# Cached keys turned by VectorE in place in an attention step: the load that feeds it, and the values beside it

## The chip, the cores and the metric

The kernel runs on 1 core of one Trainium2 chip. The metric is device time in microseconds (us), the median of the runs. Before the change it is 2017.1 us over 3 runs (2013.8 to 2017.39).

## What is computed

One step of a four-layer model for a prompt of 256 positions and for 8 samples of 8 positions each. Every layer has a mixer and then a cross attention over 256 memory positions; the change is in the attention, and there in the samples' part, whose keys and values are cached in HBM per sample.

```python
D_MODEL = 1024; DEPTH = 4; DEC_BATCH = 8; DEC_SEQ = 8; N_MEM = 256; X_HEADS = 4; X_HEAD_DIM = 256

def memory_cross_attn(x, mem_k, mem_v, w_q, w_o):
    bsz, L, _ = x.shape
    q = (x @ w_q).reshape(bsz, L, X_HEADS, X_HEAD_DIM)
    s = jnp.einsum('blhd,bmhd->bhlm', q, mem_k.astype(q.dtype)).astype(F32) * (X_HEAD_DIM ** -0.5)
    p = jax.nn.softmax(s, axis=-1).astype(x.dtype)
    o = jnp.einsum('bhlm,bmhd->blhd', p, mem_v.astype(x.dtype)).reshape(bsz, L, D_MODEL)
    return o @ w_o
...
    # in reference(): 'cache_mem_k', 'cache_mem_v' have shape (DEPTH, DEC_BATCH, N_MEM, X_HEADS, X_HEAD_DIM)
    y_sample, ... = run_trunk(x_sample, cache_mem_k, cache_mem_v, ...)
```

## The kernel before

Everything is float32. A projection's weights come in blocks of 256 columns (1024x256, four transfers of 256 KB each, issued by `put`, line 425) into four slots `raw`. ScalarE writes each half block's high part to `wh` (line 1713), GpSimd the rest to `wl` (line 1693), and TensorE makes three products per tile (lines 773, 774, 778); one such half block is called a unit. Memory keys and values of the prompt are made from `raw` directly (lines 1458 and 1467).

The order of the work on each engine is written out by hand; engines wait for each other by counted semaphores. All weights, caches and states are loaded by transfers that SyncE (SP) issues in its program order, and a wait there holds up all that is behind it.

The attention of a layer, on TensorE: the prompt's memory keys; eight query units (`project`, t = 0 to 7), each scaled out of PSUM by VectorE (line 2929); the prompt's scores (`prompt_scores`, line 1541); then the samples' scores from sixteen cached key blocks of 128 positions x 1024 columns (two blocks per sample). Since a key block comes with positions on the partitions and the product needs the columns of a head there, `turn_cache` (line 1524) turns it by eight TensorE transposes into PSUM banks 4 and 5. ScalarE copies bank 4 (line 2187) and VectorE bank 5 (in `copy`, line 2258) into one of two buffers `at_kbt`, and `cache_scores` (line 1534) multiplies. Key block n + 1 is turned ahead of the scores of block n, and the turns of the prompt's probabilities (`prompt_turn`, line 1552) stand in between:

```python
                for n in range(1, 16):
                    turn_cache(n)
                    cache_scores(n - 1)
                    if n in (5, 6, 11, 12):
                        prompt_turn(n // 8, (n - 5) % 6)
                cache_scores(15)
```

Then follow the prompt's outputs (line 1571), part of the next layer's memory values (`values`, line 1467, not in the last layer), the turn of the samples' probabilities (line 1581), and the sixteen cached value blocks (line 1602, four products each), and at last the output projection, eight units.

The 32 cached blocks of a layer (keys 0 to 15, values 16 to 31) are loaded by `cache(n)` (line 647) as one transfer of 128 rows of 4096 bytes each. They share buffers, a ring of twelve (`KB_SLOT`), plus three more: a block is issued when the block before it in its buffer has been used (`at_kb_used`). Twelve key blocks are issued ahead of the scores, the other four and the values during them, as buffers come free.

Of the kernel before, what the change touches and what calls it, by code (L numbers as in the profile page):

```python
# [26 lines left out]
P = 128  # L27
D = 1024
# [99 lines left out]
def trunk(nc, A, RES):  # L128
    with ExitStack() as ctx:
# [249 lines left out]
        at_kbt = c(2, KD, P)  # L379
# [18 lines left out]
        at_kb += [work[:, 5120:6144], work[:, 0:D], work[:, D:2 * D]]  # L398
        KB_SLOT = [n % CACHED for n in range(28)] + [CACHED, CACHED + 1, CACHED + 2, 28 % CACHED]

        def cached_count(L, n):

            return 16 * (L * KB_SLOT.count(KB_SLOT[n]) + KB_SLOT[:n + 1].count(KB_SLOT[n]))
# [10 lines left out]
        def _(sp):  # L414
# [217 lines left out]
            def attention(layer, stores=None):  # L632

                def cache(n):
# [7 lines left out]
                    elif slot == CACHED:  # L642
                        for h in range(2):
                            sp.wait_ge(*past(f"at_k_out{h}", 32 * (layer + 1)))
                    elif slot > CACHED:
                        sp.wait_ge(*past("at_cs_full", 16 * (layer + 1)))
                    sp.dma_start(at_kb[slot], src).then_inc(S(f"at_kb_in{slot}"), 16)
# [36 lines left out]
                for n in range(SQUARES, CACHED):  # L684
                    cache(n)
                if layer:
# [3 lines left out]
                    store_keys(1)  # L690
                sp.wait_ge(*past("h_ready", KD * (2 * layer + 2)))
                for n in range(EARLY, SQUARES):
                    cache(n)
# [10 lines left out]
                for n in [*range(CACHED, 16), 28, *range(16, 28), 29, 30, 31]:  # L704
                    cache(n)
# [26 lines left out]
        def _(pe):  # L732
# [16 lines left out]
            def low(half, j):  # L749
                assert units.n % 2 == half  # L750
                return wl[:, units.n // 2 % SLOTS, j, half * P:(half + 1) * P]
# [691 lines left out]
            def attention(L):  # L1443
                def memory(n):
# [10 lines left out]
                    for k in range(KD):  # L1455
                        if n == 0:
                            pe.wait_ge(*past("mem_normal", 2 * KD * L + k + 1))
                        mm = pe.matmul(ps[:, n % 4, 0:NMEM], raw[:, block % SLOTS, k, n % 2 * P:(n % 2 + 1) * P], memh[:, k, :],  # L1458
# [58 lines left out]
                def turn_cache(n):  # L1517
                    kb = cached(n)
                    for g in range(2):
                        if n:  # L1520
                            pe.wait_ge(*past(f"at_kbt{g}_ready", seen + n))
                        for j in range(4):
                            c = 4 * g + j
                            mm = pe.transpose(ps[:, 4 + g, j * P:(j + 1) * P], kb[:, c * P:(c + 1) * P], ident[:])  # L1524
                        mm.then_inc(S("at_kb_used" if g else "at_kbt_full"), 1)

                def cache_scores(n):
                    b, a = n // 2, n % 2
                    pe.wait_ge(*past("at_kbt0_ready", seen + n + 1))
                    pe.wait_ge(*past("at_kbt1_ready", seen + n + 1))  # L1530
                    at = 256 * (b // 4) + P * a
                    for c in (0, 2, 4, 6, 1, 3, 5, 7):
                        rows = slice(32 * (c // 2), 32 * (c // 2) + 32)
                        mm = pe.matmul(ps[rows, 7, at:at + P], at_qz[:, b, c, :], at_kbt[:, n % 2, c, :],
                                       start=(n == 0 and c % 2 == 0), stop=(n == 15 and c % 2 == 1), skip_group_check=True)
                    mm.then_inc(S("at_cs_full"), 1)
# [8 lines left out]
                def prompt_turn(T, g):  # L1545

                    pe.wait_ge(*past("at_pp_ready", 2 * L + T + 1))
                    if T or g:
                        pe.wait_ge(*past("at_ppt_read", 4 * L + 2 * T + g))
                    for h in range(2):  # L1550
                        for a in range(2):
                            mm = pe.transpose(ps[:, 6, (2 * h + a) * P:(2 * h + a + 1) * P], at_pp[:, 2 * g + h, a * P:(a + 1) * P], ident[:])
# [21 lines left out]
                if L < DEPTH - 1:  # L1574
                    pe.wait_ge(*past("at_kbt1_ready", seen + 16))
# [9 lines left out]
                pe.wait_ge(*past("at_kbt0_ready", seen + 16))  # L1585
# [1472 lines left out]
```

## Time and profile before

| | |
|---|---|
| runs | 2017.1 us median of 3 (2013.8 to 2017.39) |
| span of the profiled execution | 2015.7 us |
| the profiled execution's own time, beside its span | not given apart from it; the median is 1.4 us above the span |
| TensorE busy (matmul) | 1951.5 us, 97% |
| VectorE / ScalarE / GpSimd busy | 62% / 46% / 50% |
| share of the 16 DMA engines | 49.8% (queue q1), 321.49 MB |
| HBM read / written | 292.16 MB / 29.61 MB |
| samples' scores of layer 0 (lines 1524, 1534, 1552) | from 346.56 to 376.91 us |

Times in the trace count from the start of the span. A row of the chain of waits gives the start, the duration and what the end of the kernel waited for at that time; matmuls overlap, so a row there gives the time by which a group moved the chain on. A float32 matmul is two records of the trace. In a table of windows, the share is that of 16 DMA engines and GB/s what they moved together.

### The profile page before, as it was taken

How to read it: one execution, taken by the hardware profiler on the slowest of the kernel's cores; microseconds unless marked ns; L12 is line 12 of the kernel's file. 1: busy time of each engine (PE TensorE's matmuls, PEld its weight loads, DVE VectorE, ACT ScalarE, POOL GpSimd, SP SyncE). 2: the span in 40 equal slices, each digit the busy share in tenths (PEclk: the TensorE clock that was granted, in tenths of full speed). 3: DMA queues.
4: the chain of work that ended last, by engine and by line, in shares of the span. 5: the costliest groups of instructions: out<-in, count | busy, mean ns of one | idle time of the engine just before them, and what ended most of it. 6: DMA issues, size and time to landing. Idle time of an engine off the chain costs nothing.

```text
span 2015.7 us, 35615 instructions
## 1 busy us (share of the span) xinstructions
PE 1951.5 (97%) x13890; PEld 1763.9 (88%) x13890; DVE 1244.4 (62%) x2220; ACT 930.6 (46%) x1557; POOL 1008.8 (50%) x1249
## 2 busy tenths in 40 slices
PE   7999999999999999999999999999999999999997
PEld 5998989798888988897889999999998889989976
DVE  5988342426887787755147777777454157874552
ACT  3676522334555555342354444443243347674333
POOL 4776704026555655250356666566631337776602
PEclk8999999999999999999999999999999999999998
DMA  4444476535444544487353444444586344445870
GB/s 130 149 147 135 135 250 231 208 105 174 124 116 132 151 132 140 138 297 241 113 170 108 130 130 130 137 136 146 165 313 211 132 148 141 135 148 166 292 231 27
DMA packets 332615, 324.64 MB, mean 161 GB/s; under 512 B 19768, under 2 KB 313056, under 8 KB 332448
## 3 DMA queue, kind: packets, MB, share of 16 engines
q1 hardware_dynamic: 330944, 321.49, 49.8%
q8 instruction: 111, 1.82, 0.4%
q10 hardware_dynamic: 1504, 0.87, 0.2%
q14 instruction: 56, 0.46, 0.1%
HBM read 292.16 MB, written 29.61 MB: 160 GB/s over the span
## 4 chain that ended last, share of the span: by engine, by line
PE 75%; DVE 14%; ACT 5%; issue 2%; DMA 2%; POOL 1%; SPq 1%; DVEq 0%; ACTq 0%
PE ps L773 10%; PE ps L774 10%; PE ps L778 10%; PE ps L1458 5%; PE ps L1467 4%; PE ps L1261 3%; PE ps L1524 2%; PE ps L888 2%; PE ps L763 2%; PE ps L765 2%; PE ps L764 2%; ACT wh L1713 2%; DVE work L2543 2%; PE ps L1602 1%; PE ps L1541 1%
## 5 line engine op out<-in xcount | busy, mean ns | idle before, releaser
L1693 POOL TENSOR_TENSOR wl<-raw,wh 128x256 fp32r<-128x256 f32 x1216 | 1003.3, 860 | 979.1 <-ACT wh L1713 978.9
L1713 ACT ACTIVATE wh<-raw 128x1024 fp32r<-128x1024 f32 x304 | 311.8, 1053 | 202.1 <-PE ps L778 49.8
L773 PE MATMUL ps<-Hh,wh 128*128 128x320 f32 x1200 | 372.2, 324 | 2.8 <-DVE work L2563 0.9
L774 PE MATMUL ps<-Hl,wh 128*128 128x320 f32 x1200 | 360.4, 314 | 0.0
L773 PEld LDWEIGHTS ps<-Hh,wh 128*128 128x128 f32 x1200 | 230.0, 192 | 11.3 <-DVE work L2427 2.3
L774 PEld LDWEIGHTS ps<-Hl,wh 128*128 128x128 f32 x1200 | 230.4, 192 | 2.1
L2258 DVE TENSOR_SCALAR work<-ps 128x512 f32<-128x512 f32 (+8 forms) x220 | 100.3, 474 | 170.9 <-PE ps L871 39.8
L778 PE MATMUL ps<-Hh,wl 128*128 128x320 f32 x1200 | 201.1, 310 | 0.0
L778 PEld LDWEIGHTS ps<-Hh,wl 128*128 128x128 f32 x1200 | 183.2, 189 | 0.1
L773 PE MATMUL ps<-Oh,wh 128*128 128x320 f32 x512 | 152.2, 310 | 3.7 <-DVE Ol L3004 3.7
L774 PE MATMUL ps<-Ol,wh 128*128 128x320 f32 x512 | 151.1, 308 | 0.0
L763 PE MATMUL ps<-Oh,wh 128*128 128x320 f32 x400 | 125.6, 314 | 2.0 <-DVE gate_area L2563 0.9
L764 PE MATMUL ps<-Ol,wh 128*128 128x320 f32 x400 | 123.0, 308 | 0.0
L765 PE MATMUL ps<-Oh,wl 128*128 128x320 f32 x400 | 123.0, 308 | 0.0
L2315 DVE TENSOR_TENSOR work<-work 128x320 f32<-128x320 f32 x80 | 41.2, 515 | 131.9 <-ACT work L2220 105.7
L1458 PE MATMUL ps<-work,raw 128*128 128x256 f32 x512 | 113.8, 379 | 0.0
L1467 PE MATMUL ps<-raw,work 128*128 128x256 f32 x512 | 113.3, 379 | 0.0
L1467 PEld LDWEIGHTS ps<-raw,work 128*128 128x128 f32 x512 | 96.8, 190 | 13.4
L1458 PEld LDWEIGHTS ps<-work,raw 128*128 128x128 f32 x512 | 96.5, 190 | 13.5
L773 PEld LDWEIGHTS ps<-Oh,wh 128*128 128x128 f32 x512 | 96.1, 188 | 4.7 <-DVE Ol L3004 4.7
L774 PEld LDWEIGHTS ps<-Ol,wh 128*128 128x128 f32 x512 | 96.0, 187 | 0.0
L2187 ACT ACTIVATE work<-ps 128x512 f32<-128x512 f32 x64 | 38.4, 600 | 111.7 <-PE ps L1524 111.7
(439 smaller groups left out, 3922.0 us busy)
## 6 DMA issues: line engine op xcount, KB each, us to landing
raw<-rg_w_in SPq DMA_DIRECT2D x128, 256.0 KB, 3.5
raw<-hg_w_in SPq DMA_DIRECT2D x128, 256.0 KB, 4.8
raw<-ssd_w_in SPq DMA_DIRECT2D x96, 256.0 KB, 3.9
work<-cache_mem_k SPq DMA_DIRECT2D x40, 512.0 KB, 6.3
work<-cache_mem_v SPq DMA_DIRECT2D x40, 512.0 KB, 5.1
raw<-rg_w_out SPq DMA_DIRECT2D x64, 256.0 KB, 3.6
raw<-x_w_k SPq DMA_DIRECT2D x64, 256.0 KB, 3.6
raw<-x_w_v SPq DMA_DIRECT2D x64, 256.0 KB, 3.7
```

The costliest lines, as they stand in the source:

```text
L763: pe.matmul(out, high(*wi), mh, start=start, stop=False)
L764: pe.matmul(out, high(*wi), ml, start=False, stop=False)
L765: return pe.matmul(out, low(*wi), mh, start=False, stop=stop)
L773: pe.matmul(ps[:, bank, 0:n], high(half, k), mh[:, k, 0:n], start=(k == 0), stop=False)
L774: pe.matmul(ps[:, bank, 0:n], high(half, k), ml[:, k, 0:n], start=False, stop=False)
L778: mm = pe.matmul(ps[:, bank, 0:n], low(half, k), mh[:, k, 0:n], start=False, stop=(k == 7))
L1261: mm = pe.matmul(out, x[:, k, t0:t0 + P], w(k), start=(k == 0 and n == 0), stop=(k == KD - 1 and n == 2))
L1458: mm = pe.matmul(ps[:, n % 4, 0:NMEM], raw[:, block % SLOTS, k, n % 2 * P:(n % 2 + 1) * P], memh[:, k, :], start=(k == 0), stop=(k == KD - 1))
L1467: mm = pe.matmul(ps[:, bank, 256 * a:256 * a + 256], memh[:, k, a * P:(a + 1) * P], raw[:, block % SLOTS, k, :], start=(k == 0), stop=(k = ...
L1693: ins = pool.tensor_tensor(out, src, wh[:, parted(n) % HALVES, r:r + 2].bitcast(F32), ALU.subtract)
L1713: act.activation(wh[:, nx.n % HALVES], raw[:, slot, :, half * P:(half + 1) * P], ACT.Copy).then_inc(hi_ready, 1)
L2258: return ts(out, src, 1.0, None, MUL)
```

## The change

Keys. A cached key block comes as four transfers, one for each quarter (64 columns) of every head. Quarter q of a head goes to partitions 32q to 32q + 31. Partition 32q + j receives from positions 4j to 4j + 3 the 64 columns of that quarter of each head: 16 pieces of 256 bytes. VectorE then turns 32x32 blocks in place (`turn_keys`), with a step of two words between the elements of a row. After this each partition holds two columns (even and odd) of all heads, and the score product reads them as they lie. The columns of a head are thus split into even and odd instead of the first and the second 128, so the query weights and the memory-key weights are read with a step of two words as well (`by_head`, `unit_of`), and the prompt's keys are put back in order as they are copied out (`take_keys`).

Positions. The turn leaves the 128 positions of a block in the order 0, 4, 8, ..., then 1, 5, ...; so the values' transfer reads its source rows in that order, `(j a) c -> a j c` with a = 4: still one transfer of 128 rows of 4096 bytes.

Order. `turn_cache` and its two copies go. Fourteen key blocks (not twelve) have buffers ahead of the scores, since the two halves of `at_kbt` became buffers. VectorE turns two blocks behind each of the first seven query tiles, the last two in the score stage. The four turns of the prompt's probabilities go to banks 4, 5, 6, 4 and are copied out by ScalarE, not VectorE.

```diff
-        at_kbt = c(2, KD, P)
+        kb13, kb14 = c(D), c(D)
...
+        KEYS = 14
+        RING = [*range(EARLY), *range(SQUARES, CACHED), EARLY, CACHED + 1, CACHED + 2]
+        KB_SLOT = RING + RING[0:2] + RING[2:] + [CACHED] + RING[0:3]
...
+        def unit_of(v, n):
+            half = n % 2
+            if any(q <= n < q + KD for q in Q_AT):
+                return v.rearrange("p k (x e) -> p k x e", e=2)[:, :, :, half]
+            return v[:, :, half * P:(half + 1) * P]
+        def turned_keys(slot):
+            return at_kb[slot].rearrange("p (r j e) -> p r e j", j=32, e=2)
...
-                    sp.dma_start(at_kb[slot], src).then_inc(S(f"at_kb_in{slot}"), 16)
+                    if n < 16:
+                        keys = src.rearrange("(j a) (h q x) -> q j (a h) x", a=4, h=XH, q=4)
+                        for q in range(4):
+                            to = at_kb[slot][32 * q:32 * q + 32].rearrange("p (r x) -> p r x", r=4 * XH)
+                            sp.dma_start(to, keys[q]).then_inc(S(f"at_kb_in{slot}"), 16)
+                    else:
+                        sp.dma_start(at_kb[slot], src.rearrange("(j a) c -> a j c", a=4)).then_inc(S(f"at_kb_in{slot}"), 16)
...
-                for n in [*range(CACHED, 16), 28, *range(16, 28), 29, 30, 31]:
+                for n in [28, *range(KEYS, 28), 29, 30, 31]:
                     cache(n)
...
-                turn_cache(0)
                 pe.wait_ge(*past("at_qz_ready", L + 1))
-                for n in range(1, 16):
-                    turn_cache(n)
-                    cache_scores(n - 1)
-                    if n in (5, 6, 11, 12):
-                        prompt_turn(n // 8, (n - 5) % 6)
-                cache_scores(15)
+                for n in range(16):
+                    cache_scores(n)
+                    if n in (4, 12):
+                        prompt_turn(n // 8, 0)
+                        prompt_turn(n // 8, 1)
...
+                def turn_keys(n):
+                    slot = KB_SLOT[n]
+                    wait(f"at_kb_in{slot}", cached_count(L, n))
+                    dve.transpose(turned_keys(slot), turned_keys(slot)).then_inc(S("at_kb_turned"), 1)
...
                     ts(at_q[:, t], ps[:, t % 4, 0:NT], 256.0 ** -0.5, None, MUL).then_inc(S("at_q_ready"), 1)
+                    if t < KEYS // 2:
+                        turn_keys(2 * t)
+                        turn_keys(2 * t + 1)
```

TensorE's order in layer 0, from the prompt's scores on. Before (lines 1541 scores of the prompt, 1524 turns of key blocks, 1534 their scores):

```order
L1541 MATMUL ps<-work 128x256 x16
L1524 MATMUL ps<-ident,work 128x128 x16
L1534 MATMUL ps<-work 32x128 x8
L1524 MATMUL ps<-ident,work 128x128 x8
L1534 MATMUL ps<-work 32x128 x8
L1524 MATMUL ps<-ident,work 128x128 x8
L1534 MATMUL ps<-work 32x128 x8
```

And with the change (1558 scores of the prompt, 1551 scores of key blocks, 1569 turns of the prompt's probabilities, 1586 its outputs):

```order
L1558 MATMUL ps<-work 128x256 x16
L1551 MATMUL ps<-work 32x128 x40
L1569 MATMUL ps<-ident,work 128x128 x8
L1551 MATMUL ps<-gate_area,work 32x128 x8
L1551 MATMUL ps<-cache_area,work 32x128 x40
L1551 MATMUL ps<-work 32x128 x16
L1569 MATMUL ps<-ident,work 128x128 x8
L1551 MATMUL ps<-work 32x128 x24
L1586 MATMUL ps<-work 128x256 x16
```

The scores of all sixteen blocks follow each other, with the prompt's turns after the fifth and the thirteenth.

SP's order in the same place. Before (line 425 weights, 647 cached blocks, 454 and 660 results):

```order
L647 DMA cache_area<-cache_mem_k 128x1024 x5
L647 DMA work<-cache_mem_k 128x1024
L454 DMA out_mv<-work 128x2x1024
L425 DMA raw<-x_w_v 128x2x256 x4
L425 DMA raw<-x_w_o 128x2x256 x12
L647 DMA work<-cache_mem_k 128x1024 x4
L647 DMA work<-cache_mem_v 128x1024 x2
L647 DMA gate_area<-cache_mem_v 128x1024
```

And with the change (444 weights, 668 keys, 670 values, 473 results):

```order
L668 DMA cache_area<-cache_mem_k 32x16x64 x20
L668 DMA work<-cache_mem_k 32x16x64 x12
L473 DMA out_mv<-work 128x2x1024
L444 DMA raw<-x_w_v 128x2x256 x4
L444 DMA raw<-x_w_o 128x2x256 x12
L670 DMA work<-cache_mem_v 128x1x1024
L668 DMA work<-cache_mem_k 32x16x64 x8
L670 DMA work<-cache_mem_v 128x1x1024 x3
L670 DMA gate_area<-cache_mem_v 128x1x1024
```

Eight blocks stand ahead of the weights in place of six, value block 28 comes ahead of the last two key blocks, and each key block is four transfers.

VectorE's order at the end of the query units, with the change (2946 scales a query tile, 2940 turns a key block; before, the scalings followed each other):

```order
L2940 STREAM_TRANSPOSE cache_area<-cache_area 128x16x2x32
L2940 STREAM_TRANSPOSE work<-work 128x16x2x32
L2946 TENSOR_SCALAR work<-ps 128x320
L2940 STREAM_TRANSPOSE work<-work 128x16x2x32 x2
L2946 TENSOR_SCALAR work<-ps 128x320
L2270 TENSOR_SCALAR work<-work 128x2x8x8 x4
L2963 TENSOR_REDUCE smallc<-ps 128x4
```

These are the last of the seven pairs; each pair stands between two query tiles, and TensorE waits for a tile three units later. The last tile, the placing of the samples' queries (2270) and the prompt's maximum (2963) come behind all fourteen turns.

## Rows read from the trace of the kernel before

**Rows 1.** The page, busy us (share of the span) xinstructions.
```profile
PE 1951.5 (97%) x13890; PEld 1763.9 (88%) x13890; DVE 1244.4 (62%) x2220; ACT 930.6 (46%) x1557; POOL 1008.8 (50%) x1249
```
**Rows 2.** Chain of waits in layer 0, 330 to 420 us: start us, us, what.
```profile
339.39 7.17 PE ps L1541 x32
...
370.74 0.59 PE ps L1552 x4
...
372.77 1.02 PE ps L1524 x8
373.80 0.57 PE ps L1534 x16
...
376.91 7.11 PE ps L1571 x32
...
391.36 5.32 PE ps L1602 x96
...
397.05 1.91 PE ps L1602 x32
```
**Rows 3.** The same chain in the last layer, 1915 to 1975 us.
```profile
1914.84 7.17 PE ps L1541 x32
...
1952.09 7.11 PE ps L1571 x32
...
1966.83 1.91 PE ps L1602 x32
```
**Rows 4.** The DMA view: packets, then transfers xcount, KB each, us to landing.
```profile
DMA packets 332615, 324.64 MB, mean 161 GB/s; under 512 B 19768, under 2 KB 313056, under 8 KB 332448
...
work<-cache_mem_v SPq DMA_DIRECT2D x40, 512.0 KB, 5.1
...
work<-state_rglru_conv SPq DMA_DIRECT2D x16, 24.0 KB
...
out_rgc_p<-work SPq DMA_DIRECT2D x16, 3.0 KB
out_rgh_p<-work SPq DMA_DIRECT2D x16, 1.0 KB
out_rgh_s<-work SPq DMA_DIRECT2D x16, 8.0 KB
...
work<-ssd_w_in SPq DMA_DIRECT2D x1, 128.0 KB, 3.6
...
smallc<-ssd_d SPq DMA_DIRECT2D x1, 16.0 KB, 2.4
```
**Rows 5.** Windows: us, engines busy (x instructions), granted clock, DMA share, GB/s.
```profile
259.00:261.00 2.00, 2.00 (x11) 1.77 (x10) 2.00 (x6) 0.96 (x3) 0.00 (x0) 1.00 1.01 412
...
350.00:360.00 10.00, 9.18 (x127) 6.80 (x127) 7.77 (x16) 3.74 (x9) 0.00 (x0) 1.00 0.92 323
...
380.00:381.00 1.00, 1.00 (x6) 0.90 (x5) 0.00 (x0) 0.00 (x0) 0.00 (x0) 1.00 0.95 385
...
1034.00:1035.00 1.00, 1.00 (x8) 1.00 (x8) 0.00 (x0) 0.00 (x0) 1.00 (x2) 1.00 0.56 171
```
**Rows 6.** Lines 425 and 647: issue ns min/median/max; landing of cached blocks.
```profile
L425 SPq DMA_DIRECT2D raw<-rg_w_a x32: 551/609/624, 39.0 to 1781.8; - x32
...
DMA to landing us min/median/max: 3.4/5.5/12.3
```
**Rows 7.** VectorE: a query tile in order of time; the nearest operation of 1024 elements.
```profile
909.54 0.49 DVE L2929 TENSOR_SCALAR work<-ps 128x320 f32<-128x320 f32 x1 [3.03 <-PE ps L778]
...
L2567 DVE TENSOR_TENSOR work<-work 128x1024 f32<-128x1024 f32 x8 | 10.9, 1369 | 2.3 <-ACT work L1907 2.3
```
**Rows 8.** Windows near the start, columns as in rows 5.
```profile
25.00:30.00 5.00, 2.89 (x12) 1.79 (x12) 5.00 (x7) 3.49 (x8) 5.00 (x6) 1.00 0.00 0
...
40.00:42.00 2.00, 2.00 (x9) 2.00 (x9) 1.97 (x8) 1.48 (x5) 0.00 (x0) 0.50 0.26 71
42.00:44.00 2.00, 2.00 (x14) 2.00 (x13) 1.89 (x8) 1.51 (x5) 0.00 (x0) 0.84 0.70 190
```

More of the change, by code:

```diff
@@ L397, in trunk, with by_head @@
         CACHED = len(at_kb)
-        at_kb += [work[:, 5120:6144], work[:, 0:D], work[:, D:2 * D]]
-        KB_SLOT = [n % CACHED for n in range(28)] + [CACHED, CACHED + 1, CACHED + 2, 28 % CACHED]
+        at_kb += [work[:, 5120:6144], kb13, kb14]
+        KEYS = 14
+        RING = [*range(EARLY), *range(SQUARES, CACHED), EARLY, CACHED + 1, CACHED + 2]
+        KB_SLOT = RING + RING[0:2] + RING[2:] + [CACHED] + RING[0:3]
         def cached_count(L, n):
-            return 16 * (L * KB_SLOT.count(KB_SLOT[n]) + KB_SLOT[:n + 1].count(KB_SLOT[n]))
+            landings = [64 if m < 16 else 16 for m in range(32)]
+            same = [m for m in range(32) if KB_SLOT[m] == KB_SLOT[n]]
+            return L * sum(landings[m] for m in same) + sum(landings[m] for m in same if m <= n)
+        def by_head(v, half):
+            return v.rearrange("p (x e) -> p x e", e=2)[:, :, half]
+        def unit_of(v, n):
[5 more added lines that the diff above has]
+            return at_kb[slot].rearrange("p (r j e) -> p r e j", j=32, e=2)
+        TURN_BANK = (4, 5, 6, 4)
         at_m = smallc[:, 288:352].rearrange("p (a b) -> p a b", b=8)
@@ L683, in attention @@
                     query(1)
-                for n in range(SQUARES, CACHED):
+                for n in range(EARLY, EARLY + 2):
                     cache(n)
@@ L690, in attention @@
                     store_keys(1)
+                for n in range(EARLY + 2, EARLY + 5):
+                    cache(n)
                 sp.wait_ge(*past("h_ready", KD * (2 * layer + 2)))
-                for n in range(EARLY, SQUARES):
+                for n in range(EARLY + 5, KEYS):
                     cache(n)
@@ L750, in low @@
                 assert units.n % 2 == half
+                if any(q <= units.n < q + KD for q in Q_AT):
+                    return by_head(wl[:, units.n // 2 % SLOTS, j, :], half)
                 return wl[:, units.n // 2 % SLOTS, j, half * P:(half + 1) * P]
@@ L1515, in cached @@
                     return at_kb[KB_SLOT[n]]
[L1517 to L1525, printed above, removed]
                 def cache_scores(n):
                     b, a = n // 2, n % 2
-                    pe.wait_ge(*past("at_kbt0_ready", seen + n + 1))
-                    pe.wait_ge(*past("at_kbt1_ready", seen + n + 1))
+                    pe.wait_ge(*past("at_kb_turned", seen + n + 1))
+                    keys = turned_keys(KB_SLOT[n])
                     at = 256 * (b // 4) + P * a
@@ L1708, in split @@
                 n = PARTED[nx.n]
-                slot, half = n // 2 % SLOTS, n % 2
+                slot = n // 2 % SLOTS
                 act.wait_ge(landed[slot], 64 * (n // 8 + 1))
@@ L2956, in prompt_scale @@
                             ins.then_inc(S("at_pp_ready"), 1)
[L2958 to L2960 removed]
                 prompt_max(0)
[L2963 to L2979 removed]
+                prompt_scale(0)
+                prompt_max(1)
+                if L < DEPTH - 1:
+                    memory_norm(L + 1, range(0, 4))
+                prompt_scale(1)
+                for n in range(KEYS, 16):
+                    turn_keys(n)
+                if L < DEPTH - 1:
+                    memory_norm(L + 1, range(4, KD))
+                wait("at_kb_used", 32 * L + 16)
                 did(dve.tensor_reduce(at_m[:, 5, 0:2], ps[:, 7, :].rearrange("p (b m) -> p b m", b=2), axis=AX, op=MAX))
```

64 lines of the change are left out of this document (20 added, 44 removed).

## The prediction

> **What bounds the kernel now.** I read the page first. TensorE is busy 97% of the span [rows 1], so only time taken from TensorE's queue, or a wait put into it, can move the end. The change sits in the attention part, which runs four times, so next I read the chain of waits through that part of layer 0 [rows 2]. It runs on TensorE without a break: the prompt scores (L1541) end at 339.39 + 7.17 = 346.56 us. I call this moment T. Then the sixteen cached key blocks are turned (L1524) and multiplied (L1534), and at 376.91 the prompt's outputs (L1571) begin. At 391.36 the sixteen cached value blocks are multiplied (L1602), the last of them ending at 397.05 + 1.91 = 398.96. So the key blocks take 376.91 - 346.56 = 30.35 us, and the value blocks end at T + 52.4. In the last layer [rows 3] T is 1922.01 and the value blocks end at 1968.74, T + 46.7, since no memory values for a next layer stand between. Layers 1 and 2 repeat layer 0 shifted in time.
>
> **What leaves TensorE.** At its steady pace a key block costs 1.02 us of turning and 0.57 of scores, and a turn of the prompt's probabilities 0.59 [rows 2]. The order of the changed program shows the sixteen score groups and four prompt turns alone. That is 16 x 0.57 + 4 x 0.59 = 11.5 us in place of 30.35, so 18.9 us less per layer and 75 us over four. Part of it is stalls behind the copies out of the turned banks, which go too. ScalarE's sixteen copies become four and VectorE's sixteen go; both were beside TensorE's work.
>
> **What VectorE gets.** Fourteen turns of 128x1024 stand two by two behind the query tiles, and two more inside the score stage. No row shows such a turn. The nearest is another operation of the same 1024 elements, 1.37 us [rows 7]. From below I take a copy's pace, 0.49 us for 320 elements, hence 1.0 or so with the fixed part spread; from above, twice 1.37. I take 1.37, the row with the same size. Between two query tiles VectorE now works 0.49 us and idles 3.03, a period of 3.52 [rows 7]; 0.49 + 2 x 1.37 = 3.23 fits, so the turns cost nothing as long as one is under (3.52 - 0.49)/2 = 1.5 us and the key blocks have landed. The strided reads (every second word, for the q and k weights and the turned keys) I cost at nothing: ScalarE's and GpSimd's splits run ahead, and no row of a step of two says otherwise. The range has to carry this.
>
> **What the DMA queue gets.** A key block is now 2048 pieces of 256 bytes in four transfers. The rate per engine is GB/s over share over 16. It is 412/1.01/16 = 25.5 and 385/0.95/16 = 25.3 for whole 4096-byte rows at their best, 323/0.92/16 = 21.9 when all engines are crowded, and 171/0.56/16 = 19.1 for 512-byte pieces, which is 27 ns a piece [rows 5]. A 256-byte piece costs between half of that and all of it, so a block takes 1.7 to 3.5 us of all engines against 1.3 now. Fourteen blocks come before T in about 90 us, so at most 31 us of work is added to a stretch in which the engines still have room; I take no cost. Issuing is dearer: the transfers whose source rows are cut finer (128 KB, L425) take 0.609 us of SP each [rows 6], so a key block takes 2.4 us of SP. Blocks 14 and 15 are issued after T, ahead of the values.
>
> **The values are the term that decides.** Their transfer still moves 128 rows of 4096 bytes, but the source is now read as 4 groups of 32 rows, because the turned order of the positions needs it. What does that do to the engines? The packets tell. The profile counts 19768 packets under 512 bytes [rows 4]. Of these 1408 are data: 1024 pieces of 128 bytes for one ssd_w_in transfer, and 3 x 128 for ssd_d and its two like. That leaves 18360 over 1231 transfers, the sum of the counts in that view. If each transfer put one closing packet on all 16 engines there would be 19696. Suppose instead it runs on the largest number up to 16 that divides its rows: 12 for the 80 transfers of 24 rows, 8 for 32 of 8 rows, 3 for 40 of 3 rows, 1 for 16 of one row, 16 for the other 1063. This gives 960 + 256 + 120 + 16 + 17008 = 18360, exactly. So a transfer is cut along its outermost count only, in equal parts, and never inside it (one row of 1 KB stays on one engine). The new source's outermost count is 4. An equal cut of both sides along it goes to 4 engines and no further.
>
> The Trainium skill ("DMA: Bandwidth & Descriptors", section on why a DMA increments its semaphore by 16 and not by 1) says this outright: the number is the largest up to 16 that divides the slowest count of both access patterns, and they are always the lowest-numbered engines. By it the values run on the same four engines; were the on-chip side alone to count (128 rows), it would be 16 and the whole change a gain of 75 us. The trace agrees for equal counts; no row has sides that differ.
>
> **The sum.** On four engines one value block takes 131072 bytes / 25.4 GB/s = 5.16 us, and blocks queue behind each other on the same four. After T: 0.6 us until key block 0 is used, 8 issues x 0.61 = 4.9, one value issue 0.3, then the fixed part of a landing, 3.4 us at the fastest [rows 6] less its 1.3 of data = 2.1. One value block (28) goes ahead of T; the other fifteen follow: 15 x 5.16 = 77.4. With 0.5 for the last block's products the stage ends at T + 85.8. Against T + 52.4 that is +33.4 us in layers 0 to 2, against T + 46.7 it is +39.1 in layer 3: +139 together. The 18.9 us saved ahead become waiting and are lost. One more term is TensorE's clock, since it works 0.5 us of each 5 in that wait. Early in the kernel a stretch with 2.89 us busy of 5 is still granted 1.00, and later stretches show 0.50, half speed (1.2 of 2.4 GHz). The stretch 42 to 44 us has 0.84, which puts the rise at 42.6 [rows 8]. Matmuls had stood close from about 39 us, so some 3.6 us of dense work ran at half speed and lost 1.8; four times, +7. So span 2015.7 + 146 = 2162; the median of the runs lies 1.4 above the span shown, hence 2163.
>
> **Rival 1, faster: the values still use all engines** (the on-chip side decides, or successive blocks go to different fours). Then a block takes 1.3 to 1.5 us, the sixteen are there when TensorE arrives, and the layers keep 18.9 us each: 2017 - 75 = 1942. For it: rows 4 prove the cut only where both sides agree. Against it: a cut into 16 equal parts of 4 groups would have to go inside the outermost count, which 3 rows and 1 row show it doesn't. It decides from about seven engines up: (52.4 - 8.4)/15 = 2.9 us a block is break-even.
>
> **Rival 2, slower still: the turn isn't hidden.** At 2.7 us a turn, seven tiles each take 0.49 + 5.5 - 3.52 = 2.4 us longer, T comes 17 us later in each layer, and on top of the values that is 2163 + 68 = 2231. For it: no row prices the turn. Against it: it would be dearer than any elementwise row of its size.
>
> **How the numbers follow.** The four-engine case has 0.78, rival 1 0.17, rival 2 0.04, something between (a wait I don't see, near today's time) 0.01. The four-engine case's own range: down to 2140 without the fixed parts, with cheaper issues and no clock loss; up to 2213 if each engine gives only the crowded 21.9 GB/s (5.99 us a block, +12.4 a layer), a little more if small pieces hold up weights. Eight in ten is then 2125 to 2225, which leaves out rival 1 and most of rival 2. A change of 0.2%, 4 us, is about what a measurement of this kernel can tell from none; no case lands there by itself. Faster 0.17, within 0.2% 0.01, slower 0.82.
>
> **What would show it.** Right: L1524's successor gone, key scores from T to about T + 12; then TensorE waiting some 55 us a layer on the landings of the values, one block every 5.2 us, the DMA share near 0.25 with about 100 GB/s there, the granted clock at 0.50; and 153144 packets under 512 bytes: 1408, the 131072 key pieces, and 18360 + 192 x 16 (more key transfers) - 64 x 12 (values on 4 engines, not 16). On 16 engines it would be 153912. Wrong: a DMA share near 0.9 and 300 GB/s after T and no wait on values; or VectorE's turns near 2.7 us with TensorE waiting on the query tiles.

## The result and the profile after

The changed kernel took 2231.5 us (median of 4 runs, 2228.5 to 2235.4), the kernel before 2015.4 us on the same chip: a ratio of 1.107, 95% interval 1.104 to 1.109. Forecast was 2163 us, 2125 to 2225. The direction was right, the size was 68 us short and outside the range.

The page of the changed kernel, with busy shares and the shares of the chain that ended last:

```profile
span 2233.7 us, 34475 instructions
...
PE 1945.7 (87%) x13378; PEld 1736.5 (78%) x13378; DVE 1267.2 (57%) x2204; ACT 903.5 (40%) x1509; POOL 1009.8 (45%) x1249
...
PE 54%; DMA 16%; DVE 14%; SPq 8%; ACT 5%; issue 3%; ACTq 0%; DVEq 0%
```

TensorE has 512 matmuls fewer than in [rows 1] and 87% in place of 97%. A sixth of the chain that sets the end is now DMA, and 8% is SyncE's issuing. The DMA view counts the packets:

```profile
DMA packets 457794, 324.57 MB, mean 145 GB/s; under 512 B 153144, under 2 KB 446432, under 8 KB 457632
```

153144 is the number forecast for values on four engines (153912 on sixteen). So where the two sides of a transfer have unequal outermost counts, here 4 and 128, which no row of before has, the smaller one set the number. The value stage of layer 0, from the timeline of TensorE (start us, us, what, and in brackets the idle time ahead and what ended it):

```profile
394.85 1.08 PE L1614 MATMUL ps<-cache_area,work 128*32 128x256 f32 x8 [4.35 <-DMA cache_area<-cache_mem_v]
399.84 1.08 PE L1614 MATMUL ps<-cache_area,work 128*32 128x256 f32 x8 [3.91 <-DMA cache_area<-cache_mem_v]
404.83 1.08 PE L1614 MATMUL ps<-cache_area,work 128*32 128x256 f32 x8 [3.91 <-DMA cache_area<-cache_mem_v]
```

One block every 4.99 us (5.16 forecast), and TensorE waits 3.9 us of it. The windows of the same stage and of what follows, columns as in [rows 5]:

```profile
390.00:440.00 50.00, 11.87 (x90) 2.32 (x86) 0.42 (x1) 0.77 (x2) 0.00 (x0) 0.53 0.30 114
...
452.00:454.00 2.00, 2.00 (x10) 2.00 (x9) 0.00 (x0) 0.00 (x0) 2.00 (x4) 0.51 0.00 0
454.00:456.00 2.00, 2.00 (x15) 2.00 (x15) 0.00 (x0) 0.23 (x1) 2.00 (x4) 1.00 0.00 0
```

Share 0.30 (0.25 forecast), 114 GB/s (100 forecast), clock 0.53: half speed (1.2 GHz) while TensorE mostly waits. Its matmuls stand close again from 450.31 us, the clock is still 0.51 from 452 to 454, and 1.00 from 454 on.

So much was in the prediction. What was not is mostly ahead of T. The table gives for each layer the time from the attention part's first matmul (L1458, now L1485) to T, the end of the prompt's scores, and from T on; every entry is the start or end of the first or last matmul of the line named.

| | before, L0 / L1 / L2 / L3 | after, L0 / L1 / L2 / L3 |
|---|---|---|
| start to T (L1541, now L1558) | 94.4 / 68.3 / 66.6 / 66.8 | 97.6 / 80.1 / 80.2 / 80.9 |
| T to end of key scores (L1534, now L1551) | 30.4 / 30.4 / 30.4 / 30.1 | 21.5 / 15.5 / 15.2 / 15.0 |
| T to end of values (L1602, now L1614) | 52.4 / 52.4 / 52.4 / 46.7 | 98.6 / 93.2 / 91.6 / 89.8 |

T comes 3.2 + 11.7 + 13.7 + 14.1 = 42.7 us later in all. How that happens stands in the timelines of layer 1. SyncE's queue (start us, us, what it issues), where before the first five key blocks took 2.66 us:

```profile
906.54 15.35 SPq L668 DMA_DIRECT2D work<-cache_mem_k  x20
921.94 2.75 SPq L668 DMA_DIRECT2D gate_area<-cache_mem_k  x4
...
929.54 10.49 SPq L668 DMA_DIRECT2D cache_area<-cache_mem_k  x8
940.08 1.89 SPq L683 DMA_DIRECT2D out_mk<-work  x1
...
946.41 0.47 SPq L683 DMA_DIRECT2D out_mk<-work  x1
```

and VectorE's:

```profile
944.71 0.69 DVE L2270 TENSOR_SCALAR work<-ps 128x512 f32<-128x512 f32 x1 [2.38 <-DMA out_mk<-work]
953.14 0.69 DVE L2270 TENSOR_SCALAR work<-ps 128x512 f32<-128x512 f32 x1 [7.74 <-DMA out_mk<-work]
954.20 1.76 DVE L2943 MEMSET work<- 128x2048 f32 x1 [0.37 <-issue]
955.89 0.43 DVE L2946 TENSOR_SCALAR work<-ps 128x320 f32<-128x320 f32 x1
956.23 2.36 DVE L2940 STREAM_TRANSPOSE work<-work 128x1024 f32<-128x1024 f32 x2
958.51 0.45 DVE L2946 TENSOR_SCALAR work<-ps 128x320 f32<-128x320 f32 x1
...
974.41 0.45 DVE L2946 TENSOR_SCALAR work<-ps 128x320 f32<-128x320 f32 x1
```

Eight key blocks (32 transfers) stand ahead of the first two stores of new keys (out_mk). They take 15.35 + 2.75 + 10.49 = 28.6 us of SyncE's time, where in the kernel before eleven blocks stand there and take 5.8. VectorE's last copy of keys waits 7.74 us for the second store to land, so the query tiles start late, and then each takes 2.65 us with its two turns (955.89 to 958.51) until the last at 974.41, on which TensorE waits. That wait costs once more. The prompt's scores before, after, and the window in the middle of them:

```profile
913.61 7.17 PE L1541 MATMUL ps<-work 128*128 128x256 f32 x32 [0.58 <-DVE work L2929]
...
974.92 9.47 PE L1558 MATMUL ps<-work 128*128 128x256 f32 x32 [4.12 <-DVE work L2946]
...
976.00:978.00 2.00, 2.00 (x6) 1.62 (x5) 0.00 (x0) 0.92 (x1) 0.00 (x0) 0.50 1.09 350
```

TensorE had idled 4.12 us and runs at half speed (1.2 GHz) at first. In layers 2 and 3 the same scores take 8.86 us each, so 5.7 of the 42.7 us are this clock.

### The profile page after: what moved, and what is told of

Its sections match the earlier page's. It is cut to its first block, busy times and chain, and to the rows that moved or that the text cites. A ratio compares the mean times of both kernels' runs of the same rounds, so it can differ in the third digit from the quotient of the medians.

```text
span 2233.7 us, 34475 instructions
## 1 busy us (share of the span) xinstructions
PE 1945.7 (87%) x13378; PEld 1736.5 (78%) x13378; DVE 1267.2 (57%) x2204; ACT 903.5 (40%) x1509; POOL 1009.8 (45%) x1249
## 2 busy tenths in 40 slices
DMA packets 457794, 324.57 MB, mean 145 GB/s; under 512 B 153144, under 2 KB 446432, under 8 KB 457632
## 4 chain that ended last, share of the span: by engine, by line
PE 54%; DMA 16%; DVE 14%; SPq 8%; ACT 5%; issue 3%; ACTq 0%; DVEq 0%
DMA work<-cache_mem_v 9%; PE ps L800 8%; PE ps L801 7%; PE ps L805 7%; SPq L668 5%; DMA cache_area<-cache_mem_v 4%; PE ps L1494 3%; PE ps L1288 3%; PE ps L790 2%; SPq L444 2%; PE ps L792 2%; PE ps L791 2%; ACT wh L1724 2%; DVE work L2423 2%; DVE work L2555 1%
## 5 line engine op out<-in xcount | busy, mean ns | idle before, releaser
L800 PE MATMUL ps<-Oh,wh 128*128 128x320 f32 x512 | 160.9, 325 | 8.9 <-DVE work L2946 3.9
L801 PE MATMUL ps<-Ol,wh 128*128 128x320 f32 x512 | 158.5, 321 | 0.0
L790 PE MATMUL ps<-Oh,wh 128*128 128x320 f32 x400 | 126.6, 317 | 2.0 <-DVE gate_area L2575 0.9
L2270 DVE TENSOR_SCALAR work<-ps 128x64 f32<-128x64 f32 (+7 forms) x140 | 45.6, 353 | 145.7 <-DMA out_mk<-work 41.6
L791 PE MATMUL ps<-Ol,wh 128*128 128x320 f32 x400 | 123.8, 310 | 0.0
L1614 PE MATMUL ps<-work 128*32 128x256 f32 x320 | 36.7, 561 | 97.7 <-DMA work<-cache_mem_v 96.5
L1485 PE MATMUL ps<-work,raw 128*128 128x256 f32 x512 | 113.8, 379 | 0.0
L800 PEld LDWEIGHTS ps<-Oh,wh 128*128 128x128 f32 x512 | 102.1, 199 | 12.4 <-DVE Ol L3014 5.3
L1485 PEld LDWEIGHTS ps<-work,raw 128*128 128x128 f32 x512 | 99.6, 196 | 10.5
L1494 PEld LDWEIGHTS ps<-raw,work 128*128 128x128 f32 x512 | 96.7, 190 | 14.1 <-ACT work L2147 0.6
```

The lines of the kernel that those rows point to most:

```text
L790: pe.matmul(out, high(*wi), mh, start=start, stop=False)
L791: pe.matmul(out, high(*wi), ml, start=False, stop=False)
L800: pe.matmul(ps[:, bank, 0:n], high(half, k), mh[:, k, 0:n], start=(k == 0), stop=False)
L801: pe.matmul(ps[:, bank, 0:n], high(half, k), ml[:, k, 0:n], start=False, stop=False)
L1485: mm = pe.matmul(ps[:, n % 4, 0:NMEM], by_head(raw[:, block % SLOTS, k, :], n % 2), memh[:, k, :], start=(k == 0), stop=(k == KD - 1))
L1494: mm = pe.matmul(ps[:, bank, 256 * a:256 * a + 256], memh[:, k, a * P:(a + 1) * P], raw[:, block % SLOTS, k, :], start=(k == 0), stop=(k = ...
```

## The experiments

All times are medians of 4 or more runs beside the kernel before (2015 to 2020 us); intervals are of the ratio. In e2, e3, e5, e8, e11 and e13 keys or values lie out of place, so they do the same work on other numbers and serve for timing alone. "T" in the text is the time from start to T, mean over layers 1 to 3: 67.2 us before, 80.4 after.

**The values alone, both ways.** In the changed kernel, one transfer over all rows, with ScalarE writing the probabilities in the natural order:

```diff
-    sp.dma_start(at_kb[slot], src.rearrange("(j a) c -> a j c", a=4)).then_inc(...)
+    sp.dma_start(at_kb[slot], src).then_inc(...)
...
-    act.activation(at_p[:, hb, :], ps[:, 7, ...], ACT.Exp, ...)
+    act.activation(at_p[:, hb, :].rearrange("p (h j a) -> p h a j", h=2, a=4),
+                   ps[:, 7, ...].rearrange("p (h a j) -> p h a j", h=2, a=4), ACT.Exp, ...)
```

> The changed kernel with its value blocks read in natural order again, as one transfer of 128 source rows; ScalarE puts the samples' probabilities back in order of position as it writes them (same instructions, a step of four words in the write). Theory A (a source read as 4 groups of rows runs on 4 DMA engines, and the values queue there): the 53 us a layer of waiting on values go, TensorE waits on no value load, the DMA share after T is again near 0.9, packets under 512 bytes are 153912 and not 153144, time 1985 to 2010 us (what is left is the later T, 43 us together, against 15 us or so a layer saved in the score stage). Rival B (values are late because SP issues them late, behind eight key transfers and a full queue, whatever their shape): still 30 us or more a layer of waiting on values, time over 2150 us.

And in the kernel before, only the values as 4 groups of 32 rows:

> The kernel before with only the value blocks' source read in 4 groups of 32 rows. The positions of the values no longer agree with the probabilities (the samples' attention is another sum); same work. Theory A: value stage ends about T + 92 instead of T + 52 in layers 0 to 2 and about 45 us later in layer 3, with TensorE's clock at half in the wait: 2170 to 2200 us, a value block every 5 us, DMA share 0.25. Rival B (only the issue and the key pieces matter): 2010 to 2025 us.

Measured: 1993.2 us, ratio 0.988 (0.986 to 0.991), and 2203.5 us, ratio 1.092 (1.089 to 1.094). The source access of sixteen value blocks a layer is worth 238 us in the one kernel (2231.5 - 1993.2) and 185 in the other (2203.5 - 2018.4 beside it). e1 fell in its range, e2 4 us above its own. In e1 TensorE waits for no value load: 22 to 24 us from the end of the key scores to the end of the values in layers 0 to 2 (77 in the changed kernel). A value block's issue, median 0.434 us (in the changed kernel 4.8, about what the block before it needs on four engines):

```profile
L670 SPq DMA_DIRECT2D work<-cache_mem_v x40: 327/434/1692, 348.9 to 1938.4; - x40
```

The changed kernel:

```profile
L670 SPq DMA_DIRECT2D work<-cache_mem_v x40: 528/4792/10187, 349.4 to 2159.6; - x40
```

**The keys alone.** The kernel before with only the loading of the keys changed: four transfers of 256-byte pieces on 32 partitions each (e3), or four transfers of 32 whole rows (e6).

```diff
-    sp.dma_start(at_kb[slot], src).then_inc(S(f"at_kb_in{slot}"), 16)
+    keys = src.rearrange("(j a) (h q x) -> q j (a h) x", a=4, h=XH, q=4)
+    for q in range(4):
+        to = at_kb[slot][32 * q:32 * q + 32].rearrange("p (r x) -> p r x", r=4 * XH)
+        sp.dma_start(to, keys[q]).then_inc(S(f"at_kb_in{slot}"), 16)
```

for e3, and for e6

```diff
+    for q in range(4):
+        sp.dma_start(at_kb[slot][32 * q:32 * q + 32], src[32 * q:32 * q + 32]).then_inc(...)
```

> The kernel before with only the key blocks' transfers exchanged for the four of 256-byte pieces each; what lies in the buffers is no longer a block of keys in TensorE's layout, so the samples' scores are of other numbers; same work. Theory: the later start of the scores (42 us over the four layers in the changed kernel) comes from SP, which takes 0.63 us a transfer and holds the query weights and the copies of the keys behind them: twelve key blocks ahead instead of fourteen, so 25 to 40 us slower, 2040 to 2055 us, with T later by 8 to 12 us in layers 1 to 3. Rival (VectorE's turns and their waits make T late): 2010 to 2025 us.

> The kernel before with each key block as four transfers of 32 whole rows of 4096 bytes: four issues, no small pieces. If the number of transfers alone costs (SP busy with issues), near e3: 2035 to 2055 us. If the pieces cost (512 of them to be named per transfer, 18 to 25 ns each on an engine), it stays within 10 us of before, and a transfer is issued in 0.33 to 0.45 us instead of 0.63.

Measured: 2069.2 us, 1.024 (1.021 to 1.027), and 2042.8 us, 1.013 (1.010 to 1.015). T rose to 83.9 and 75.5. So the keys' loading does cost, with no turn on VectorE at all, and more than e3's theory named (25 to 40 us, T later by 8 to 12); about half of it comes with whole rows, by the number of transfers and the 32 partitions. In layer 0 neither moved T (94.4).

**Is it SyncE's order?** e4 takes e1 and puts six key blocks, the query weights and two stores first, the other keys later; e8 is e4 with short turns; e7 is e4's order with the values on four engines; e5 is e1 with short turns. The order of SyncE for layers 1 to 3, and the short turn:

```diff
+    query(1); store_keys(0); query(2); query(3); store_keys(1)
+    keys(6, 9)
+    put(cols_of(A["x_w_v"][layer + 1], 0)); keys(9, 11)
+    put(cols_of(A["x_w_o"][layer], 0)); keys(11, 13)
...
-    dve.transpose(turned_keys(slot), turned_keys(slot))
+    dve.transpose(at_kb[slot][:, 0:32], at_kb[slot][:, 0:32])
```

> The changed kernel with the cached values in one transfer each on 16 engines (as in e1_values16), and with SyncE's order of issues changed too: in layers 1 to 3 only six key blocks stand ahead of the query weights and of the first two stores of the new keys, in layer 0 the keys 6 to 9 stand one by one between the query weights, and the last key blocks stand between the output weights. Theory S (the late end of the prompt's scores T is SyncE's queue: fourteen key blocks of four transfers at 0.63 us stand ahead of what VectorE and ScalarE wait for): T comes 3 to 5 us sooner in layer 0 and 10 to 15 us sooner in layers 1 to 3 than in e1_values16, start to T near 95, 68 to 70, 67 to 70, 67 to 70 us, time 1945 to 1965 us. Rival D (the 256-byte pieces crowd the DMA engines, whatever the order): T hardly moves, time within 10 us of e1_values16's 1993 us. Rival V (VectorE's turns between the query tiles pace TensorE): T moves by under half of that, 1975 us or more.

> e1_values16 with each in-place turn cut to the first 32 of 1024 elements of a row (the key scores are then those of keys that are not turned). It takes about 1.1 us per turn from VectorE and nothing from any other engine. Theory S alone: VectorE's turns fit between the query tiles, T and the time stay within 5 us of e1_values16 (1993 us). Rival V: once the query tiles start late, VectorE needs 0.38 + 2.27 us a tile and hands them over late; with short turns it catches up at 0.4 us a tile, T comes 8 to 15 us sooner in layers 1 to 3 and the time is 1950 to 1970 us.

> The changed kernel with SyncE's order of e4_order, but with the cached values still read as 4 groups of 32 rows, on 4 engines. Theory: the value blocks (5.0 us each) set the end of the stage, and they are issued at the same place behind the output weights, so an earlier T gives back only what the first value block comes sooner: start to T falls by 3 to 15 us a layer as in e4_order, and start to values end by about as much, since the whole queue moves forward; 2180 to 2200 us against 2231 of the changed kernel. If the landings of values are tied to something other than SyncE's place, the waiting grows by what T gains, and the time stays within 10 us of 2231.

> e4_order with the short turns of e5_short_turn (keys not turned). Theory S: with the order mended VectorE's turns hide behind the query tiles (1.22 us each, two per 3.52 us tile), so the time is within 4 us of e4_order's. Rival V: some 5 us or more a layer sooner, 20 us or more in all.

Measured: e4 2019.5 us, 1.001 (1.000 to 1.003; one of its ten runs took 6232 us); e5 1980.6, 0.984 (0.979 to 0.988); e7 2240.1, 1.111 (1.109 to 1.114); e8 2007.6, 0.996 (0.995 to 0.998). The reordering was my theory's test and it failed: T rose from e1's 81.0 to 87.2. The second store of new keys now landed 7 to 9 us sooner in layers 1 to 3, and VectorE waited for the keys themselves, 13 to 14 us a layer ahead of T where it had waited 0 in e1. In the whole run (e4):

```profile
DVE work L2950 <- DMA work<-cache_mem_k: 50.2, 17, 6.0
```

In this order the fourteen blocks and the weights did not fit ahead of T either; no other order was tried. e5 shows that the turns take part, by less than rival V said (8 to 15 us): T fell to 73.7. That is 7.3 us a layer, and 2.2 of it is the clock, since the prompt's scores took 8.86 to 9.66 us in e1 and 7.17 in e5. About half of the 7.3 came back behind T, where the score stage grew by 1.8 to 4.5 us. With e4's order short turns gave 12 us (e8, T 86.3), between the 4 and the 20 that the two theories named. In e7, too, T is late (87.4) and the values end 88.8 us after it, so its expectation of 2180 to 2200 us fell with that of e4.

**Is it SyncE's issue time at all?** e11 is e3 with six of its twelve early blocks issued from ScalarE (the expectation's fourteen is the changed kernel's number), e9 and e10 are e1 with six and three.

```diff
+    def cache_keys(n):                      # in ScalarE's program, for the same blocks
+        act.wait_ge(*past("at_area", L + 1))
+        act.wait_ge(*past("y_added", Y_DONE[L]))
...
+            act.dma_start(to, keys[q]).then_inc(S(f"at_kb_in{slot}"), 16)
```

> e3_before_pieces (the kernel before with each cached key block in four transfers of 256-byte pieces, its scores those of rows put together otherwise) with six of the fourteen key blocks ahead of T issued from ScalarE instead of SyncE. The DMA engines get the same pieces; SyncE gets 24 transfers, about 15 us, less ahead of T. Theory S (SyncE's issue time put T off by 15 to 17 us in layers 1 to 3): T comes back to within 4 us of the kernel before (start to T 94, 68 to 72, 67 to 71 us), time 2015 to 2030 us. Rival D (the pieces crowd the DMA engines or the queue behind them): T stays 10 us or more late and the time stays above 2050 us. ScalarE pays about 2.4 us per block it issues, in gaps.

> e1_values16 with the same six key blocks issued from ScalarE. Theory S: T comes 8 to 15 us sooner in layers 1 to 3 and some 3 us in layer 0; VectorE's turns then fit between the query tiles; time 1945 to 1965 us. Rival D: no change beyond 10 us from 1993. Rival V (the turns pace the query tiles even with everything on time): T comes at most half as much sooner, 1975 us or more.

> e1_values16 with three key blocks issued from ScalarE in place of six (8 us less on SyncE ahead of T). Theory S: about half of what e9_act_issue gains, 1965 to 1980 us. If ScalarE's own issuing costs something on the path, this one is the faster of the two.

Measured: e11 2052.4 us, 1.017 (1.015 to 1.020), T 79.2 against e3's 83.9; e9 1994.5, 0.989 (0.986 to 0.992); e10 1992.6, 0.989 (0.987 to 0.991), both as e1. Theory S missed in all three: only 4.7 of 16.7 us came back in e11 and nothing in the other two. Rival D's marks were met (e11 above 2050 us with T 12.0 us late, e9 within 10 us of 1993). One 10 us window, while the first key blocks load, says more. e3, one queue:

```profile
861.00:871.00 10.00, 10.00 (x50) 8.80 (x49) 8.20 (x18) 3.96 (x10) 0.00 (x0) 1.00 1.34 173
```

e11, two queues:

```profile
860.00:870.00 10.00, 10.00 (x47) 8.71 (x47) 7.41 (x17) 3.76 (x10) 0.00 (x0) 1.00 1.37 174
```

The engines give 173 to 174 GB/s of 256-byte pieces at a share above 1, whoever issues; a block of 524288 bytes needs 3.0 us at that. The Trainium skill ("DMA: Bandwidth & Descriptors", section on queues, rings and completion order) says that SP and ACT each own one ring on the same 16 engines; the trace agrees, 174 against 173 GB/s.

**SyncE's time without the engines'.** e12 loads each block in two transfers of 256-byte pieces over 128 partitions, e13 in four of 512-byte pieces, e15 in one large transfer and eight tiny ones of sixteen 64-byte pieces. The edit of e15:

```diff
+    sp.dma_start(at_kb[slot][:, 0:D - 16], src[:, 0:D - 16]).then_inc(...)
+    for r in range(0, P, 16):
+        sp.dma_start(at_kb[slot][r:r + 16, D - 16:D], src[r:r + 16, D - 16:D]).then_inc(...)
```

> The kernel before with each cached key block in two transfers instead of one, over all 128 partitions, each of every second 256-byte piece of the rows: the pieces have the size of the change, SyncE issues half as many transfers as e6_before_rows4. Theory D (the time that 256-byte pieces take of the DMA engines, which are full for the first 40 us of the stage in layers 1 to 3, puts T off): start to T near 80 to 84 us in layers 1 to 3 and 94 in layer 0, a rate of 170 to 190 GB/s while keys are loaded, time 2055 to 2070 us. Theory S (SyncE's issuing): SyncE spends under 10 us more ahead of T than before, T moves by under 4 us, time 2015 to 2030 us.

> e3_before_pieces with pieces of 512 bytes in place of 256, still four transfers of 32 partitions each (key scores of rows put together otherwise). Theory D: the rate while keys load lies between the 173 GB/s of 256-byte pieces and the 245 GB/s of whole rows on 32 partitions; T is put off by 10 to 14 us in layers 1 to 3; time 2045 to 2060 us. Theory S: as many transfers, T as late as in e3_before_pieces if their issue time stays at 0.63 us, 2065 us.

> The kernel before with each cached key block in nine transfers: one of 128 pieces of 4032 bytes and eight of 16 pieces of 64 bytes. SyncE gets about 3.0 us of issuing per block, as much as with the 256-byte pieces of e3_before_pieces (3.05), while the DMA engines get some 0.3 us per block more than before instead of 1.5. Theory S (SyncE's issue time puts T off): start to T near 84 us in layers 1 to 3, time 2060 to 2070 us. Theory D (engine time of the pieces): T within 4 us of before, time 2015 to 2030 us. Half and half, as e11_before_pieces_act suggests: 2030 to 2045 us.

Measured: e12 2049.8 us, 1.016 (1.013 to 1.019); e13 2051.0, 1.018 (1.013 to 1.023); e15 2108.5, 1.046 (1.042 to 1.049). e13 came as theory D said. e12 missed both ranges: T is 10.9 us late where D said 13 to 17 and S under 4. SyncE's time on the five blocks that are first in layer 1 was

```profile
854.87 12.30 SPq L652 DMA_DIRECT2D work<-cache_mem_k  x10
```

or 2.5 us a block, but this is not the price of issuing. The shortest, median and longest issue of the same line (ns):

```profile
L652 SPq DMA_DIRECT2D work<-cache_mem_k x80: 550/1107/3144, 254.8 to 1961.0; - x80
```

The first of a burst of such transfers takes 0.55 us; the later ones take about 1.1, with the engines at a share above 1, and even the value block behind the last burst of layer 1 takes 1.08 us to issue where 0.33 is usual in that kernel. So SyncE is held up by full engines. Its own part would be some 2 x 0.55 = 1.1 us a block, and yet T is 10.9 us late: e12 speaks for theory D. e15 shows that theory S can hold too. SyncE:

```profile
869.71 0.41 SPq L650 DMA_DIRECT2D work<-cache_mem_k  x1
870.17 3.67 SPq L652 DMA_DIRECT2D work<-cache_mem_k  x8
873.88 0.42 SPq L650 DMA_DIRECT2D work<-cache_mem_k  x1
```

and the same stretch in the windows:

```profile
873.00:883.00 10.00, 10.00 (x48) 8.76 (x47) 8.18 (x19) 5.00 (x12) 0.00 (x0) 1.00 0.55 153
```

A block costs SyncE 4.2 us (873.88 - 869.71; 3.0 expected), the engines are half idle, and T is 93.6: SyncE's time alone can put T off. Beside each other, with SyncE's time, held up or not, from the five blocks that are first in layer 1:

| kernel | SyncE us a block | GB/s, share while keys load | T later, layers 1 to 3 |
|---|---|---|---|
| before | 0.53 | 380, 1.03 | 0 |
| e6, 4 x 32 rows | 1.9 | 245, 1.05 | 8.2 |
| e12, 2 x 1024 pieces of 256 B | 2.5 | 216, 1.07 | 10.9 |
| e13, 4 x 256 pieces of 512 B | 2.6 | 206, 1.21 | 12.2 |
| e3, 4 x 512 pieces of 256 B | 3.05 | 173, 1.34 | 16.7 |
| e15, 1 + 8 tiny | 4.2 | 153, 0.55 | 26.4 |

Eleven blocks stand ahead of the stores in all six. Eleven times the added SyncE time, less some 7 to 14 us that SyncE had to spare, gives the last column. In e3 the two limits lie close together: SyncE needs 4 x 0.63 = 2.5 us a block, the engines 3.0, and SyncE's 3.05 is that of a queue held up by full engines. That is why moving issues to ScalarE gave back little. The price of 32 partitions apart from that of more transfers in e6 was not tried.

**Fewer keys ahead of T.** e14 is e1 with ten blocks loaded and turned ahead of T, four behind the output weights.

> e1_values16 with ten key blocks loaded and turned ahead of T instead of fourteen; the four others are loaded behind the output weights and turned in the score stage. Theory D: 4 x 2.9 us of engine time leave the crowded stretch; T comes 3 to 10 us sooner in layers 1 to 3, but the score stage waits for the late blocks and their turns and grows by 3 to 12 us; the sum is open, 1975 to 2010 us. Theory V (the turns between the tiles pace): T comes sooner by up to 7 us in layers 1 to 3 as in e5_short_turn, and the score stage grows by about 4 x 1.22 us less what it waits for anyway.

Measured: 2007.8 us, 0.995 (0.994 to 0.997). T fell to 73.5, 7.6 less than in e1, but the key scores ended 20 to 22 us after it instead of 12 to 15, so the time is 15 us above e1's. Both theories had named such a fall of T, so e14 doesn't part them.

**The early value block.** e16 is the changed kernel with value block 28 issued behind keys 14 and 15.

```diff
-    for n in [28, *range(KEYS, 28), 29, 30, 31]:
+    for n in [*range(KEYS, 29), 29, 30, 31]:
```

> The changed kernel with the one early value block (28) issued behind key blocks 14 and 15 instead of ahead of them. Theory: that block lies on four engines for 5 us and holds the keys behind it there, so the scores end at T + 12 to 13 us instead of T + 15; the values then follow as sixteen blocks of 5.0 us instead of fifteen, so the stage ends 2 to 5 us later; time 2235 to 2255 us. If the chain of value blocks doesn't set the stage's end, the time falls by the 3 us a layer that the scores gain, 2220 us.

Measured: 2235.7 us, 1.107 (1.103 to 1.111), no difference from the changed kernel that can be told. The scores end at T + 11.8, 11.9 and 12.5 in layers 1 to 3 (15.5, 15.2 and 15.0 with the block ahead), the values at 92 to 94: its 5 us on four engines held the keys, but the values' own chain sets the end.

The fastest complete kernels are e1, e10 and e9, level with each other at 0.988 to 0.989 of the kernel before.

## Why the prediction missed

**The values** held in kind. Four engines, 5.0 us a block, the packets, the share, the clock: all as worked out; e1 and e2 show that this alone turns a gain into a loss. From the end of a layer's values to the next start (to the kernel's end in layer 3) it took 2.6, -2.3, 3.2 and 2.5 us more than before, 6.0 in all, where I had put 7 on the clock. Only the third stands clear: kernels that have all engines for the values differ among themselves by 5 us in the first of these stretches, 13 in the second, 3 in the third and 3 in the last, and the third is 1 us above the longest of them. That 6 lies so near 7 is in part luck.

**The step that failed is the keys' DMA work**, "at most 31 us of work is added to a stretch in which the engines still have room; I take no cost". With it fails the second term put at nothing, the turns. Together they cost 42.7 us ahead of T, where the sum has 0. In e1, where T comes 46.1 us later over the four layers, e5 divides them: 21.9 us stay with short turns, so the load alone does that much, and 24.2 go with the turns, 8.2 of these by TensorE's clock. In the kernel before the load without turns costs more (50 us in e3, where eleven blocks stand ahead of the stores). The bounds of the piece price held: 3.0 us a block lies between 1.7 and 3.5. The room did not exist where it was needed. In layers 1 to 3 the engines of the kernel before are full while the first eleven blocks load:

```profile
862.00:872.00 10.00, 10.00 (x50) 8.81 (x49) 8.52 (x19) 4.28 (x11) 0.00 (x0) 1.00 1.03 380
872.00:882.00 10.00, 10.00 (x49) 8.71 (x49) 7.57 (x10) 6.92 (x15) 6.46 (x8) 1.00 1.02 373
```

and the stage is 67 us long there, not the 90 that I took from layer 0, the only layer in which T hardly moved. The SyncE price (2.4 us a block) was in the text as well, and I never laid it along the queue: 8 x 2.4 - 5.8 = 13 us more ahead of a store that VectorE waits for; with the engines full it came to 28.6 - 5.8 = 23.

**The turn** took 1.225 us, not 1.37, and so by my own bound of 1.5 it should have cost nothing. The bound supposed query tiles that arrive at TensorE's pace of 3.52 us. With VectorE late, the tiles are all there and it catches up at 2.65 us a tile, where the scaling alone takes 0.45. Whether the turns are free with the load on time, as the bound says, no run shows. The strided reads, also costed at nothing, did no harm that shows: a split takes ScalarE 1.15 us in place of 1.06 in layer 0, and GpSimd is busy 1009.8 us in all, 1008.8 before.

**The end of the values** was T + 85.8 and came at T + 98.6, 93.2, 91.6 and 89.8: 30 us in all too early. In layer 1 eight issues of keys 14 and 15 took 9.37 us where I took 4.9:

```profile
985.05 9.37 SPq L668 DMA_DIRECT2D work<-cache_mem_k  x8
994.46 1.77 SPq L670 DMA_DIRECT2D work<-cache_mem_v  x3
```

because value block 28 was still on its four engines: with it behind the keys (e16) they took 5.27. The last three value blocks of that layer come 5.4 to 6.3 us apart and not 5.0, beside the last output weights. In layer 0 ScalarE was held besides, by output weights that stood behind 32 key transfers, 24.0 us of SyncE's time where six transfers had taken 3.8; from the chain of waits:

```profile
343.28 6.55 DMA raw<-x_w_o
...
350.82 1.04 ACT wh L1724
351.87 1.83 ACT work L2186 x8
```

The probabilities of the prompt (L2186) stand behind that split in ScalarE's program.

Neither miss alone leaves the range: by subtraction the time is some 2189 without the 42.7 us and some 2201 without the 30. The account of the stages closes: 139 forecast for the values, 42.7 ahead of T, 30 behind it and 6.0 of clock make 217.7; the spans differ by 2233.7 - 2015.7 = 218.0.

**The rivals.** Rival 1, all engines, was refuted by the packets; e1 shows what it was worth, 1993 us and not 1942, since 46 us ahead of T are lost there too. Rival 2 named 2231 us, the time measured, but by a mechanism that isn't there: a turn of 2.7 us. Its place, VectorE between the query tiles, was nearer the truth than I gave it.

## What to carry to other kernels

A piece of a change that is called hidden has to be laid along each queue that it passes, in the layer with the least room, and not summed against the average: the issuing engine's time and the DMA engines' time are two limits, and here each was enough by itself (e15 the first, e12 the second). Before transfers are cut finer or regrouped, look at the outermost count: regrouping the source of sixteen value blocks a layer cost 238 us here and 185 in the kernel before, and the same positions could be had by writing the probabilities in another order. Slack measured with engines on time is gone when one of them starts late; what counts then is how fast it catches up, and whether TensorE's clock falls while it waits.

## What was not expected of the hardware

- Issue time follows neither the bytes nor the number of pieces alone. Medians: 0.33 us for a cached value block of 128 rows of 4 KB before, 0.42 for one of its key blocks there and for one of 16 pieces of 64 bytes (e15), 0.61 for 256 pieces of 512 bytes (e13), 0.63 for 512 of 256 bytes (e3). 1024 pieces of 256 bytes (e12) took 0.55 at the least and 1.11 in the median, with the engines full.
- When the queue is full, SyncE itself stands: a value block's issue took 4.8 us, as long as the block before it needs on its four engines. All that follows in SyncE's program waits with it.
- The same 4 KB rows move at 380 GB/s in one transfer over 128 partitions and at 245 GB/s in four over 32, at the same DMA share (1.03 and 1.05; windows of 10 us that hold query weights too).
- A wait of 4.12 us of TensorE ahead of the prompt's scores came with a granted clock of 0.50 for their first part, 2.3 us lost in layer 1.
